# Spreading the background sums of weights differently over the slots of POOL's queue, in a fused encoder step

## The chip, the cores and the metric

One core of one Trainium2 chip runs the whole program in one launch. The metric is the device time in microseconds (us), the median of the runs shown. Engines are named as in the profile: PE (TensorE), DVE (VectorE), ACT (ScalarE), POOL (GpSimd), SP (SyncE, which here only issues DMAs).

## What is computed

One layer of a hybrid encoder for 512 prompt tokens and 32 tokens of a running stream, 544 in all, 1024 features, float32:

```python
xn = rms_norm(x, g_mix)
u, q, k, v, gates = split(xn @ w_in)               # one projection, 4096 columns
y_pool = multiscale_pool(u)                        # causal window means 2/4/8/16, minus the token
y_sb = stick_breaking(q, k, v)                     # 8 heads of 64, strictly causal
merged = sig(gate_a) * (y_pool @ w_pool_up) + sig(gate_b) * (y_sb @ w_sb_up)
x = x + merged @ w_out
x = x + square(relu(rms_norm(x, g_mlp) @ w_up)) @ w_down      # D_FF = 4096
x = x + sigmoid(rms_norm(x, g_ple) @ w_ple_gate) * (p @ w_ple_proj)
y = rms_norm(x, g_final)
```

## The kernel before, in words

Activations stay on chip, features on the partitions, 544 tokens along the free dimension. Weights come from HBM in tiles of 128 x 1024 float32 (512 KB), and each is split by ACT (the rounded part, w_hi, L845 and L853) and DVE (the rest, w_lo, L1812 and L1820), so that three PE products stand for one float32 product. SP loads the tiles (L651 up to the output projection, L680 to L690 behind it). Until the MLP there are two raw buffers, and ACT and DVE split three tiles ahead of PE.

**Stages.** Four "pairs" come first: each projects eight weight tiles (PE L1345, L1348, L1351) and runs two attention heads in between. Then come the mixer (the pooling and attention outputs projected up, the sample tokens' attention), the output projection, the MLP in four chunks, and the gated embedding.

**A head.** For head g PE makes the scores (L1381), ACT the softplus chain (L921 to L925), DVE closes it (L1898). POOL then zeroes what is not causal in four 128x128 blocks (mask_diagonals, L767, counted in spm_done). ACT and DVE split the masked matrix (L930, L1913), and PE sums it (L1394). ACT takes the exponential (L938). POOL masks it again (L767, counted in pm_done), ACT and DVE split it (L943, L1919), and PE multiplies it by v (L1420). Every engine's program is in order. In the same queues stand the weight splits and the q, k and v parts of the next pair.

**The background sums.** From the MLP on, groups of weights are multiplied in a Strassen-Winograd form: seven products stand for eight, and four of the seven left operands are sums of quarters of the weights (S1 to S4). POOL makes these sums with DMAs from HBM to HBM, in the Internal tensor sums_t: a plain copy (L782), and transfers that add to their destination (accumulate, L789). Each of the 16 groups (SUM_GROUPS: up 0, up 1, dn 0, dn 1, up 2, ..., ple 1) takes four steps (SUM_STEPS): four copies, then two additions, then one, then one, each transfer 512 KB, 128 in all. Steps are run in slots. Slot k first waits until every transfer of the slots before it has landed (sum_copies, a wait on sums_in for sums_made(k - 1)), then issues its copies and its additions. Slots 0 to 7 stand in POOL's queue right behind the second mask of heads 0 to 7. For even heads the pooling branch's window_sums (L742 to L747) stand between the two masks. Its window_mean (L757 to L760) stands behind the slot, but for head 6, where it stands ahead of the second mask. Slots 8 to 18 follow the heads; but for slot 8 they are paced by PE's progress (paces, waits on full). In the kernel before, group i begins in slot i. SP loads a sum of group i only when the slot of its last step has landed (L679).

Of the kernel before, what the change touches and what calls it, by code (L numbers as in the profile page):

```python
# [19 lines left out]
HEADS = 8  # L20
# [66 lines left out]
SUM_STEPS = ((("S1", "A21"), ("S3", "A21"), ("S2", "A11"), ("S4", "A12")), (("S1", "A22"), ("S3", "A11")),  # L87
             (("S2", "S1"),), (("S4", "S2"),))

SUM_GROUPS = tuple((what, 2 * c + e) for c in range(CHUNKS) for what in ("up", "dn") if what == "up" or c < SEVENS  # L90
                   for e in range(2)) + (("ple", 0), ("ple", 1))

SUM_PAD = 16

# [63 lines left out]
def t_dn(c, s, e):  # L158
    return T_MLP + c * T_CHUNK + 2 * T_UP + 2 * s + e


def t_down(c, q):
    return T_MLP + c * T_CHUNK + 2 * T_UP + q


def t_ple(g, s):
    return T_PLE + g * (T_UP + 1) + PLE_PLACE[g][s]


def t_group(g, s):  # L170
    return t_up(g, s) if g < UP_GROUPS else t_ple(g - UP_GROUPS, s)
# [31 lines left out]
def group_side(name):  # L203

    if name[0] == "dn":
        return ("dn", 2 * name[1] + name[3]), SIDES[name[2]]
    if name[0] in ("down", "proj", "p"):
        return None
    g, what = name
    return ("up", g) if g < UP_GROUPS else ("ple", g - UP_GROUPS), what  # L210


def stored_tile(name):

    if name[0] == "down":
        return T_MLP + 16 * name[1] + 8 + name[2]
    if name[0] == "proj":
        return T_MLP + 16 * CHUNKS + 5 * name[1] + 4
    (stage, g), what = group_side(name)
    return quarter_tile(stage, g, what)  # L220
# [77 lines left out]
def hybrid_step_kernel(nc, w_tiles, x_t, p_t, ck_t, cv, state_t, w_grp, vecs,  # L298
# [5 lines left out]
    with ctx:  # L304
# [3 lines left out]
        def sem(name):  # L308
            return ctx.enter_context(nc.semaphore(name))
# [156 lines left out]
        def raw_at(n):  # L466

            return (n + RAW_RING) % RAW_BUFS

        def raw_buf(n):  # L470
            b = raw_at(n)
            return raw[:, b, :] if b < RAW_RING else raw_more[:, b - RAW_RING, :]
# [23 lines left out]
        def tokens(i):  # L496
            return slice(i * HALF, (i + 1) * HALF)
# [24 lines left out]
        sums_in = sem("sums_in")  # L522
# [98 lines left out]

        def sum_slot(k):

            return [(i, k - i) for i in range(max(0, k - len(SUM_STEPS) + 1), min(k + 1, len(SUM_GROUPS)))]

        def sums_made(k):

            return 16 * sum(len(SUM_STEPS[step]) for j in range(k + 1) for _, step in sum_slot(j))
# [7 lines left out]
        @block.sync  # L636
        def _(sp):

            first = (("w", 0), ("x", 0), ("w", 2), ("x", 1), ("x", 2), ("x", 3), ("w", 1), ("x", 4), ("w", 3),
                     ("x", 5), ("x", 6), ("x", 7))  # L640
            for what, n in first:
                if what == "x":
                    sp.dma_start(xt[:, n, :], x_t[n, :, :]).then_inc(x_in[n], 16)
                else:
                    t, part = n // 2, slice(n % 2 * D_MODEL // 2, (n % 2 + 1) * D_MODEL // 2)
                    sp.dma_start(raw[:, t, part], w_tiles[t, :, part]).then_inc(half_in[n] if n < 3 else raw_in[1], 16)

            with sp.Fori(1, T_OUT // RAW_RING + 1) as r:
                for s in range(RAW_RING):
                    sp.wait_ge(wlo_done, r * RAW_RING + (s - RAW_RING + 1))  # L650
                    sp.dma_start(raw[:, s, :], w_tiles[r * RAW_RING + s, :, :]).then_inc(raw_in[s], 16)  # L651

            def wait_free(n):

                if n < RAW_BUFS - RAW_RING:
                    sp.wait_ge(yblo_done, 2)
                elif n < RAW_BUFS:
                    sp.wait_ge(wlo_done, T_MLP - RAW_RING + raw_at(n) + 1)
                else:
                    name = STAGED_LOADS[n - RAW_BUFS]  # L660
                    if name[0] == "dn":
                        sp.wait_ge(wlo_done, t_dn(*name[1:]) + 1)
                    elif name[0] == "down":
                        sp.wait_ge(wlo_done, t_down(name[1], name[2]) + 1)
                    elif name[0] == "p":
                        sp.wait_ge(ptlo_done, name[1] + 1)
                    elif name[0] == "proj":
                        sp.wait_ge(wlo_done, t_ple(name[1], T_UP) + 1)
                    else:
                        g, what = name  # L670
                        sp.wait_ge(wlo_done, t_group(g, SIDES.index(what)) + 1)

            def staged(n):
                name = STAGED_LOADS[n]
                wait_free(n)
                group, what = group_side(name) or (None, None)
                if what in SUMS:
                    nth = SUM_GROUPS.index(group)
                    sp.wait_ge(sums_in, sums_made(nth + len(SUM_STEPS) - 1))  # L679
                    sp.dma_start(raw_buf(n), sums_t[len(SUMS) * nth + SUMS.index(what), :, :])\  # L680
                        .then_inc(raw_in[raw_at(n)], 16)
                elif name[0] == "p":
                    sp.dma_start(raw_buf(n)[:, 0:TOK], p_t[:, name[1], :]).then_inc(raw_in[raw_at(n)], 16)
                else:
                    sp.dma_start(raw_buf(n), w_tiles[stored_tile(name), :, :]).then_inc(raw_in[raw_at(n)], 16)


            for j, t in enumerate(range(T_OUT + RAW_RING, T_MLP)):
                sp.wait_ge(wlo_done, t - RAW_RING + 1)
                sp.dma_start(raw[:, t % RAW_RING, :], w_tiles[t, :, :]).then_inc(raw_in[t % RAW_RING], 16)  # L690
                for n in range(2 * j, min(2 * j + 2, RAW_BUFS - RAW_RING)):
                    staged(n)
            for n in range(RAW_BUFS - RAW_RING, len(STAGED_LOADS)):
                staged(n)
            for nth, i in enumerate((1, 0)):

                for m in (4, 2, 0, 6) if nth else (0, 4, 2, 6):
                    if m == 0:
                        sp.wait_ge(fin_pool, 2 * nth + 2)
                    else:  # L700
                        sp.wait_ge(fin_done, len(BY_DVE) * nth + BY_DVE.index(m) + 1)
                    for two in range(2):
                        sp.dma_start(y_t[m + two, :, tokens(i)], xt[:, m + two, tokens(i)]).then_inc(out_done, 16)
            sp.wait_ge(out_done, 16 * 2 * KT)

        @block.gpsimd
        def _(pool):
# [67 lines left out]
            def sum_copies(k):  # L775

                if 0 < k:
                    pool.wait_ge(sums_in, sums_made(k - 1))
                for i, step in sum_slot(k):
                    if step == 0:  # L780
                        for what, of in SUM_STEPS[0]:
                            pool.dma_start(sum_tile(i, what), sum_tile(i, of)).then_inc(sums_in, 16)  # L782

            def sum_additions(k):

                for i, step in sum_slot(k):
                    if step:
                        for what, of in SUM_STEPS[step]:
                            pool.dma_start(sum_tile(i, what), sum_tile(i, of), accum_op=ALU.add).then_inc(sums_in, 16)  # L789
# [21 lines left out]
            paces = [(0, 0), (N_ATT, N_ATT + KT // 2), (N_OUT, N_OUT + KT // 2)]  # L811
            for c in range(CHUNKS):
                second = [NTH[("dn", c, s, 0)] for s in (0, 4)] if c < SEVENS else [NTH[("down", c, q)] for q in (0, 4)]
                paces += [(NTH[("up", 2 * c, 0)], NTH[("up", 2 * c + 1, 0)]), tuple(second)]
            for k, (copies, additions) in enumerate(paces, HEADS):
                if copies:
                    pool.wait_ge(full, copies)
                sum_copies(k)
                if copies:
                    pool.wait_ge(full, additions)  # L820
                sum_additions(k)
# [1732 lines left out]
```

## Time and profile before

| what | value |
|---|---|
| time, median of 3 runs | 772.89 us (772.16 to 772.94) |
| the profiled execution | 772.34 us, its span 770.6 us |
| granted TensorE clock, mean | 0.996 of full speed |
| PE busy | 754.8 us, 98% of the span |
| DVE, ACT, POOL busy | 556.9, 422.0, 147.2 us |
| DMA from POOL (q0) | 67.18 MB, 35.5% of 16 engines' span |
| DMA from SP (q1) | 94.16 MB, 35.6% |

The profile takes one execution. Busy PE includes matmuls that overlap in the pipeline, so its idle time is the safer reading: a few stretches at the start and the end, and hardly any between. The DMA engines' share is a mean over stretches with very different traffic.

### The profile page before, as it was taken

How to read it: one execution, taken by the hardware profiler on the slowest of the kernel's cores; microseconds unless marked ns; L12 is line 12 of the kernel's file. 1: busy time of each engine (PE TensorE's matmuls, PEld its weight loads, DVE VectorE, ACT ScalarE, POOL GpSimd, SP SyncE). 2: the span in 40 equal slices, each digit the busy share in tenths (PEclk: the TensorE clock that was granted, in tenths of full speed). 3: DMA queues.
4: the chain of work that ended last, by engine and by line, in shares of the span. 5: the costliest groups of instructions: out<-in, count | busy, mean ns of one | idle time of the engine just before them, and what ended most of it. 6: DMA issues, size and time to landing. Idle time of an engine off the chain costs nothing.

```text
span 770.6 us, 14459 instructions
## 1 busy us (share of the span) xinstructions
PE 754.8 (98%) x5902; PEld 746.2 (97%) x5902; DVE 556.9 (72%) x705; ACT 422.0 (55%) x524; POOL 147.2 (19%) x259
## 2 busy tenths in 40 slices
PE   9999999999999999999999999999999999999994
PEld 9999999999999999999999999999999999999993
DVE  6776556566567527588998669965998667677986
ACT  7545535435485442477674347634763356556575
POOL 1051342453471332021110111111101000000001
PEclk9999999999999999999999999999999999999998
DMA  7254848769779899988797989789776957342503
GB/s 242 93 181 140 233 147 224 225 193 262 218 179 265 259 242 275 292 267 262 213 299 270 236 329 251 282 232 354 207 243 201 278 185 217 105 117 66 204 1 116
DMA packets 49516, 165.78 MB, mean 215 GB/s; under 512 B 6320, under 2 KB 8368, under 8 KB 49456
## 3 DMA queue, kind: packets, MB, share of 16 engines
q1 hardware_dynamic: 28512, 94.16, 35.6%
q0 software_dynamic: 18688, 67.18, 35.5%
q10 hardware_dynamic: 2256, 3.60, 1.4%
q8 instruction: 43, 0.70, 0.4%
q14 instruction: 17, 0.14, 0.1%
HBM read 160.39 MB, written 71.63 MB: 301 GB/s over the span
## 4 chain that ended last, share of the span: by engine, by line
PE 90%; DVE 5%; ACT 3%; issue 1%; DMA 1%; SPq 0%; POOL 0%; POOLq 0%; DVEq 0%
PE psum L1646 23%; PE psum L1697 16%; PE psum L1345 14%; PE psum L1351 14%; PE psum L1348 14%; PE psum L1394 1%; PE psum L1422 1%; DMA xt<-x_t 1%; PE psum L1420 1%; PE psum L1382 1%; PE psum L1381 1%; ACT xt L1265 1%; PE psum L1401 1%; PE psum L1406 1%; ACT L879 0%
## 5 line engine op out<-in xcount | busy, mean ns | idle before, releaser
L853 ACT ACTIVATE w_hi<-raw_more 128x1024 fp32r<-128x1024 f32 x83 | 87.7, 1056 | 72.3 <-PE psum L1697 43.3
L1345 PE MATMUL psum<-a_hi,w_hi 128*128 128x272 f32 x576 | 120.6, 291 | 0.6 <-DVE w_lo L1812 0.5
L1820 DVE TENSOR_TENSOR w_lo<-raw_more,w_hi 128x1024 fp32r<-128x1024 f32 x83 | 101.1, 1222 | 26.1 <-ACT w_hi L853 25.7
L1351 PE MATMUL psum<-a_hi,w_lo 128*128 128x272 f32 x576 | 119.3, 289 | 0.0
L1348 PE MATMUL psum<-a_lo,w_hi 128*128 128x272 f32 x576 | 118.9, 288 | 0.0
L1646 PE MATMUL psum<-u_hi,w_hi 128*128 128x272 f32 x560 | 116.4, 289 | 1.0 <-ACT h_of L1097 1.0
L1646 PE MATMUL psum<-u_hi,w_lo 128*128 128x272 f32 x560 | 115.8, 289 | 0.0
L1646 PE MATMUL psum<-u_lo,w_hi 128*128 128x272 f32 x560 | 115.7, 288 | 0.0
L1345 PEld LDWEIGHTS psum<-a_hi,w_hi 128*128 128x128 f32 x576 | 90.3, 189 | 1.1 <-DVE w_lo L1812 0.7
L1348 PEld LDWEIGHTS psum<-a_lo,w_hi 128*128 128x128 f32 x576 | 90.5, 189 | 0.0
L1351 PEld LDWEIGHTS psum<-a_hi,w_lo 128*128 128x128 f32 x576 | 90.0, 189 | 0.0
L1646 PEld LDWEIGHTS psum<-u_hi,w_hi 128*128 128x128 f32 x560 | 87.9, 188 | 1.7 <-issue 1.2
L1646 PEld LDWEIGHTS psum<-u_lo,w_hi 128*128 128x128 f32 x560 | 88.3, 189 | 0.0
L1646 PEld LDWEIGHTS psum<-u_hi,w_lo 128*128 128x128 f32 x560 | 87.4, 188 | 0.0
L1812 DVE TENSOR_TENSOR w_lo<-raw,w_hi 128x1024 fp32r<-128x1024 f32 x41 | 51.2, 1250 | 43.3 <-ACT w_hi L845 43.1
L1820 DVE TENSOR_TENSOR w_lo<-raw,w_hi 128x1024 fp32r<-128x1024 f32 x44 | 53.6, 1222 | 19.2 <-ACT w_hi L853 12.3
L789 POOL DMA_DIRECT2D sums_t<-sums_t x32 | 27.5, 1013 | 207.1 <-PE psum L1646 87.9
L1348 PE MATMUL psum<-b_lo,w_hi 128*128 128x272 f32 x304 | 62.9, 288 | 0.0
L853 ACT ACTIVATE w_hi<-raw 128x1024 fp32r<-128x1024 f32 x39 | 41.2, 1056 | 36.0 <-PE psum L1697 21.6
L1345 PE MATMUL psum<-b_hi,w_hi 128*128 128x272 f32 x288 | 60.0, 290 | 0.0
L782 POOL DMA_DIRECT2D sums_t<-w_tiles x64 | 33.6, 535 | 135.5 <-DMA sums_t<-w_tiles 97.7
L1351 PE MATMUL psum<-b_hi,w_lo 128*128 128x272 f32 x288 | 59.4, 287 | 0.0
(287 smaller groups left out, 1553.0 us busy)
## 6 DMA issues: line engine op xcount, KB each, us to landing
sums_t<-w_tiles POOLq DMA_DIRECT2D x96, 512.0 KB, 8.2
raw<-w_tiles SPq DMA_DIRECT2D x63, 512.0 KB, 4.4
raw_more<-sums_t SPq DMA_DIRECT2D x42, 512.0 KB, 5.8
raw_more<-w_tiles SPq DMA_DIRECT2D x41, 512.0 KB, 4.5
sums_t<-sums_t POOLq DMA_DIRECT2D x32, 512.0 KB, 11.1
raw<-sums_t SPq DMA_DIRECT2D x22, 512.0 KB, 6.0
xt<-x_t SPq DMA_DIRECT2D x8, 272.0 KB, 5.7
y_t<-xt SPq DMA_DIRECT2D x16, 136.0 KB, 1.9
```

What stands on the lines that cost most here:

```text
L782: pool.dma_start(sum_tile(i, what), sum_tile(i, of)).then_inc(sums_in, 16)
L789: pool.dma_start(sum_tile(i, what), sum_tile(i, of), accum_op=ALU.add).then_inc(sums_in, 16)
L853: act.activation(w_hi[:, t % W_RING, :, :].rearrange("p k c -> p (k c)"), src, ACT.Copy)\
L1265: act.activation(x, x, ACT.Copy, scale=g_fin[:, m:m + 1]).then_inc(xg_last, 1)
L1345: pe.matmul(base[:, h, :], w_hi[:, s, wk, :], at(hi, k, h * HALF, (h + 1) * HALF), start=(opens and q == 0), stop=False, skip_group_check= ...
L1348: pe.matmul(base[:, h, :], w_hi[:, s, wk, :], at(lo, k, h * HALF, (h + 1) * HALF), start=False, stop=False, skip_group_check=True)
L1351: mm = pe.matmul(base[:, h, :], w_lo[:, s, wk, :], at(hi, k, h * HALF, (h + 1) * HALF), start=False, stop=(closes and q == len(ks) - 1), s ...
L1381: pe.matmul(z, b_lo[:, keys], b_hi[:, both], start=(b != 3), stop=False, skip_group_check=True)
L1646: mm = pe.matmul(out[:, two, :], w_part[:, t % W_RING, 2 * k + two, :], u_part[:, op, k, :], start=(OPENS[s] and k == 0 and w_part is w_hi ...
L1697: mm = pe.matmul(out[:, two, :], w_part[:, t % W_RING, 2 * k + two, :], h_part[:, i * HALF:(i + 1) * HALF], start=(OPENS[s] and k == 0 and ...
L1812: dve.tensor_tensor(w_lo[:, s, :, :].rearrange("p k c -> p (k c)"), raw[:, t % RAW_RING, :], w_hi[:, s, :, :].rearrange("p k c -> p (k c)" ...
L1820: dve.tensor_tensor(w_lo[:, t % W_RING, :, :].rearrange("p k c -> p (k c)"), src, w_hi[:, t % W_RING, :, :].rearrange("p k c -> p (k c)"), ...
```

## The change

A table BEGINS says in which slot each group begins, in place of its own number. Groups 0 to 8 begin in slots 0, 1, 2, 2, 3, 3, 4, 5, 5, groups 9 and 10 in slots 7 and 9, and groups 11 to 15 in their own slots 11 to 15, as before. The last step of each group stays three slots behind its first, and the waits follow the table. The 128 transfers are the same ones. Slots 0 to 18 stand where they stood, each with its wait for the slot before.

```diff
+BEGINS = (0, 1, 2, 2, 3, 3, 4, 5, 5, 7, 9, 11, 12, 13, 14, 15)
+SLOTS = BEGINS[-1] + len(SUM_STEPS)
...
         def sum_slot(k):
 
-            return [(i, k - i) for i in range(max(0, k - len(SUM_STEPS) + 1), min(k + 1, len(SUM_GROUPS)))]
+            return [(i, k - at) for i, at in enumerate(BEGINS) if 0 <= k - at < len(SUM_STEPS)]
...
                     nth = SUM_GROUPS.index(group)
-                    sp.wait_ge(sums_in, sums_made(nth + len(SUM_STEPS) - 1))
+                    sp.wait_ge(sums_in, sums_made(BEGINS[nth] + len(SUM_STEPS) - 1))
...
-            for k, (copies, additions) in enumerate(paces, HEADS):
+            for k, (copies, additions) in zip(range(HEADS, SLOTS), paces):
```

Transfers of each slot, copies + additions, counted from the code:

| slot | 0 | 1 | 2 | 3 | 4 | 5 | 6 | 7 | 8 | 9 | 10 | 11 |
|---|---|---|---|---|---|---|---|---|---|---|---|---|
| before | 4+0 | 4+2 | 4+3 | 4+4 | 4+4 | 4+4 | 4+4 | 4+4 | 4+4 | 4+4 | 4+4 | 4+4 |
| after | 4+0 | 4+2 | 8+3 | 8+6 | 4+7 | 8+6 | 0+7 | 4+3 | 0+4 | 4+1 | 0+3 | 4+1 |

## Rows read from the trace of the kernel before

**Rows 1.** The page: TensorE's busy time and share of the span.

```profile
PE 754.8 (98%) x5902; PEld 746.2 (97%) x5902; DVE 556.9 (72%) x705; ACT 422.0 (55%) x524; POOL 147.2 (19%) x259
```

**Rows 2.** PE's waits: who waited for what, us in total, times, longest.

```profile
PE psum L1345 <- issue: 1.1, 1, 1.1
PE psum L1646 <- ACT h_of L1097: 1.0, 1, 1.0
```

**Rows 3.** POOL's timeline in heads 2 to 7 (start, us, instructions; idle before).

```profile
111.51 2.07 POOL L782 DMA_DIRECT2D sums_t<-w_tiles  x4
...
140.45 2.15 POOL L782 DMA_DIRECT2D sums_t<-w_tiles  x4
...
152.17 1.95 POOL L767 TENSOR_SCALAR_AFFINE_SELECT work<-work 128x128 f32<-128x128 f32 x4 [6.14 <-DVE work L1898]
...
169.95 2.09 POOL L782 DMA_DIRECT2D sums_t<-w_tiles  x4
...
177.35 1.18 POOL L760 TENSOR_TENSOR upad<-gates,upad 128x559 f32<-128x559 f32 x1
183.69 1.03 POOL L767 TENSOR_SCALAR_AFFINE_SELECT work<-work 128x128 f32<-128x128 f32 x4 [5.16 <-DVE work L1898]
...
198.88 2.16 POOL L782 DMA_DIRECT2D sums_t<-w_tiles  x4
...
210.60 1.95 POOL L767 TENSOR_SCALAR_AFFINE_SELECT work<-work 128x128 f32<-128x128 f32 x4 [6.14 <-DVE work L1898]
...
228.33 2.16 POOL L782 DMA_DIRECT2D sums_t<-w_tiles  x4
...
244.37 1.02 POOL L767 TENSOR_SCALAR_AFFINE_SELECT work<-work 128x128 f32<-128x128 f32 x4 [10.46 <-DVE work L1898]
...
256.03 2.09 POOL L782 DMA_DIRECT2D sums_t<-w_tiles  x4
...
267.74 0.44 POOL L807 TENSOR_SCALAR_AFFINE_SELECT work<-work 32x256 f32<-32x256 f32 x1 [6.18 <-DVE work L2111]
```

**Rows 4.** Slots 0 to 3 to landing: stretch, engines' busy, PEclk, DMA share, GB/s.

```profile
52.90:62.40 9.50, 9.50 (x73) 9.23 (x71) 5.18 (x5) 4.63 (x5) 6.35 (x8) 1.00 0.85 300
...
82.00:98.70 16.70, 16.70 (x131) 16.53 (x131) 10.61 (x16) 9.06 (x10) 7.08 (x14) 1.00 0.93 262
98.70:102.00 3.30, 3.30 (x29) 3.30 (x28) 3.30 (x3) 1.20 (x2) 2.49 (x2) 1.00 0.12 37
111.50:129.60 18.10, 18.10 (x143) 17.93 (x141) 10.67 (x14) 8.65 (x8) 8.71 (x15) 1.00 0.95 258
...
140.40:163.00 22.60, 22.60 (x179) 22.43 (x178) 14.91 (x20) 10.29 (x11) 13.26 (x18) 1.00 0.95 254
```

**Rows 5.** POOL's timeline behind the heads: slots 8, 9 and 10.

```profile
280.25 2.09 POOL L782 DMA_DIRECT2D sums_t<-w_tiles  x4 [4.04 <-DMA sums_t<-w_tiles]
...
303.32 2.07 POOL L782 DMA_DIRECT2D sums_t<-w_tiles  x4 [17.57 <-DMA sums_t<-w_tiles]
...
330.50 1.57 POOL L782 DMA_DIRECT2D sums_t<-w_tiles  x3 [21.71 <-DMA sums_t<-w_tiles]
```

**Rows 6.** Behind head 5's first mask: ACT's and DVE's timelines, and PE's chain.

```profile
184.75 1.27 ACT L930 ACTIVATE b_hi<-work 128x1280 fp32r<-128x1280 f32 x1 [3.79 <-POOL work L767]
...
194.32 0.72 DVE L1857 TENSOR_TENSOR ev<-psum,rn 128x544 f32<-128x544 f32 x1 [0.20 <-PE psum L1351]
...
196.60 1.24 ACT L938 ACTIVATE work<-psum 128x1280 f32<-128x1280 f32 x1 [0.24 <-PE psum L1394]
...
200.28 1.49 DVE L1919 TENSOR_TENSOR b_lo<-work,b_hi 128x1280 fp32r<-128x1280 f32 x1
...
202.63 0.24 PE psum L1420
```

**Rows 7.** The page: POOL's DMA queue, its packets, MB, share of 16 engines.

```profile
q0 software_dynamic: 18688, 67.18, 35.5%
```

**Rows 8.** Weight loads (L651): to landing, from 129 to 140 us, then 141 to 163.

```profile
DMA to landing us min/median/max: 3.5/3.8/4.2
...
DMA to landing us min/median/max: 3.5/8.4/8.7
```

## The prediction

> **What bounds the kernel now.** I read the page first: PE is busy for 754.8 of 770.6 us [rows 1]. Then PE's own waits, where the reader should look for a DMA or a weight tile: between the first weights and the last stage PE waits 1.1 us once for its own issue and 1.0 us once for ACT [rows 2], and the list names no load and no sum. So even if the change frees all the DMA time between the heads and the MLP, at most 2.1 us can come back there, and neither wait names a DMA. The question is what it puts into the heads. POOL's timeline answers that [rows 3]: slots 3 to 7 are issued at 140.45, 169.95, 198.88, 228.33 and 256.03, some 29.2 us apart, and none has to wait for the slot before it, since their eight transfers have landed by then. In slot 3 the DMA engines are busy for 0.95 of 22.6 us [rows 4]. Some 6.5 us are left over per head.
>
> A difference of less than 0.2% (1.5 us) can't be told from no change.
>
> **What a slot costs.** The stretches to landing are 9.5, 16.7, 18.1 and 22.6 us for 4+0, 4+2, 4+3 and 4+4 transfers (copies + additions), weight loads between them included [rows 4]; behind slot 1 the share falls to 0.12, so the stretch ends where I put it. Four additions take 22.6 - 9.5 = 13.1 us, 3.3 us each. A copy takes at most 9.5 / 4 = 2.4; I leave 1.1 us for the start of a slot and take 2.1. Check: 4+2 gives 1.1 + 8.4 + 6.6 = 16.1 (16.7 in the row), 4+3 gives 19.4 (18.1). Then:
> - slot 2, 8+3: 1.1 + 16.8 + 9.9 = 27.8 us
> - slots 3 and 5, 8+6: 1.1 + 16.8 + 19.8 = 37.7 us
> - slot 4, 4+7: 1.1 + 8.4 + 23.1 = 32.6 us
> - slot 6, 0+7: 1.1 + 23.1 = 24.2 us
>
> **When the slots start.** Slot 2 starts at 111.5 and has landed at 139.3, 1.1 us before slot 3: no wait. Slot 3 starts at 140.45 and lands at 178.2, but slot 4 is due at 169.95, so POOL waits 8.2 us. Slot 4 lands at 178.2 + 32.6 = 210.8 (slot 5 was due at 198.9), slot 5 at 210.8 + 37.7 = 248.5 (slot 6 at 228.3), slot 6 at 248.5 + 24.2 = 272.7 (slot 7 at 256.0).
>
> **What stands behind the waiting POOL.** Its issues take 2.15 us for four [rows 3], 0.54 each; the additions I price the same. In the same rows:
> - Slot 3 issues 14 in 7.6 us, until 148.0; head 4's first mask is at 152.17. Nothing is late.
> - Slot 4: 178.2, 11 issues (5.9), and window_mean. The latter ended at 177.35 + 1.18 = 178.5, which is 8.6 us behind 169.95 with eight issues (4.3) in between, so it takes 4.3 itself. Head 5's first mask comes at 188.4, not 183.7: 4.7 late.
> - Slot 5: 210.8 + 14 x 0.54 = 218.4, for head 6's first mask at 210.6: 7.8 late in all, 3.1 more than before it.
> - Slot 6: 248.5 + 3.8 = 252.3, for head 7's at 244.4: 7.9.
> - Slot 7: 272.7 + 7 x 0.54 = 276.5, for the sample tokens' mask (L807) at 267.7: 8.8.
> These are not added up: each is measured against the unshifted time, so the largest is the total.
>
> **Does a late mask reach PE?** The chain behind head 5 [rows 6]: ACT takes the masked matrix at 184.75, when POOL releases it. Behind it in DVE's queue is the next pair's k (L1857), for which DVE sat idle for just 0.20 us; ACT's exponential (L938) had sat idle for 0.24. DVE's split ends at 200.28 + 1.49 = 201.77, and PE uses it at 202.63: 0.86 us. So the chain has some 0.9 us to give, perhaps 0.3 less at the sample tokens' mask. I take 8.8 - 1.0 = 7.8 us on PE. Each late mask also holds up the weight splits behind it in ACT's and DVE's queues; they are part of the same chain, and I add nothing.
>
> **The rest.** Weight loads: with the queue empty they land in 3.8 us, beside the sums in 8.4 (medians) [rows 8]. In the new kernel the queue is hardly empty from 111 to 290 us, so about one load of four takes 4.6 us more. Two raw buffers are loaded ahead, and while POOL is late ACT's use of them is too, so I take nothing, and 2 us at the worst. The loads behind the heads meet fewer sums (4+1 in slot 9 where 4+4 stood); since PE waited for none of them, that gives nothing. SP's waits for finished sums (L679) come true in the same slots as before or in earlier ones (group 4 in slot 6, before in slot 7; groups 11 to 15 unchanged), and the first sums, of slots 3 and 4, land at 178 and 211 us, long before the MLP.
>
> **Sum.** 772.34 (the profiled execution, 0.55 us below the median) + 7.8 = 780.1; against the median 780.7. I give 780.5.
>
> **Bounds of the one unshown price**, a slot of 11 or 14 transfers. From below: the queue's 128 transfers take 35.5% of 770.6 = 273.6 us of the engines, 2.14 each [rows 7]. Slot 3 would take 22.6 + 6 x 2.14 = 35.4, slot 4 29.0, slot 5 35.4, slot 6 20.5: then slot 4 starts at 175.9 (mask 2.4 late), slot 5 at 204.9 (1.9 late), slot 7 at 260.8 (nothing late). That is 2.4 us late, and 1.4 past the slack: 774.3. From above: slots 8 and 9 of eight transfers took 303.32 - 280.25 = 23.1 and 330.50 - 303.32 = 27.2 us, and slot 7 took 24.2 [rows 3, 5]. By 24.2 / 22.6 = 1.07 slots 3 to 6 take 141.5 instead of 132.2: 9.3 us more, 789.8. By 27.2 / 22.6 = 1.2 it would be 27 us more, 807. The slots to price run in the heads, where slot 3 stands, so I keep to its 22.6. A gain is excluded by nothing but rows 2: 2.1 us.
>
> **The rivals.**
> - **More in flight hides the waits, no change.** The rows have the engines 0.95 busy with eight transfers [rows 4], which speaks against it. It would hold if that share is mostly waiting for receipts that overlap with more transfers: 14 would then have to land in under 29.5 us, 2.1 us each, against 2.8 in slot 3. 772.9. The Trainium skill says so in "DMA: Bandwidth & Descriptors", in the anatomy of a DMA from GpSimd: a fixed 2.0 us, mostly the write's receipt, plus bytes over 436 GB/s. By that page, as an estimate, 14 transfers behind one another with one receipt take 2 + 14 x 1.2 = 18.8 us, and no slot would be late. Slot 3's eight took 22.6 us, where the page's estimate is 11.6, so the trace doesn't agree.
> - **The slack is larger than it looks.** PE's sums (L1394) of head 5 began some 5 us later than the mask allowed. If the queues' reordering gives that slack to the rest, only lateness over 6 us counts: 8.8 - 6 = 2.8, and the time 775.7; by the lower price 774.3.
> - **The queue chokes.** With 14 outstanding, POOL's issue may itself block, or the transfers slow as in slot 9 [rows 5]; POOL is then late by 18 us or more, as in the 1.07 case, and the time 790 to 807.
> - **Faster: the relief counts.** If the two PE waits [rows 2] are held by DMA traffic (the 1.1 us of issue stands at the end of the pairs) and the slots land within 29 us (2.1 us each, as above), the time is 770.8 to 771.5. It decides only if no slot is late.
>
> **How the numbers follow.** The chain of late masks 0.66; the larger slack or the lower price 0.12; the choked queue 0.12; no change 0.07; faster 0.03. Slower has 0.66 + 0.12 + 0.12 = 0.90. The range goes from 774.5 (about the lower price) to 789.0 (just under the 1.07 case); outside it lie the same, the faster, and the worst of the choke, about 0.18.
>
> **What would show it.** In the profile after: POOL's L782 (and L789 in slot 6, which has no copies) waiting for DMA sums_t in heads 4 to 7, by 8, 5 to 8, 12 and 9 us; L767 idle no longer before heads 5 and 6; ACT's L930 waiting for L767 longer, PE with new waits on DVE's b_lo (L1913, L1919) or w_lo, some 8 us in all, between 188 and 280 us; DMA share about 1.0 from 112 to 290 us and lower from 290 to 360; the MLP's stretches as long as before. It is wrong if slot 3 lands before 170 us, if L767 is late and PE doesn't wait, or if PE's new waits lie behind the heads.

## The result and the profile after

The changed kernel takes 798.26 us (median of 6 runs, 797.25 to 799.65), the kernel before 773.88 in the same comparison. The ratio is 1.0313, with a 95% interval of 1.0288 to 1.0338: slower by 3.1%. I had forecast slower, but 780.5 us, and the time lies outside my range. The profiled execution takes 798.11 us, its span 796.4, 25.8 more than before. Line numbers from here on are those of the changed kernel, 4 higher than before: the slots' copies are L786, their additions L793, the masks L771, window_mean ends in L764. In the runs further down an edit can shift them by a few lines more.

First POOL's timeline of the changed kernel, in heads 4 to 7; it answers to [rows 3].

```profile
178.61 2.09 POOL L786 DMA_DIRECT2D sums_t<-w_tiles  x4 [8.56 <-DMA sums_t<-w_tiles]
...
188.56 1.18 POOL L764 TENSOR_TENSOR upad<-gates,upad 128x559 f32<-128x559 f32 x1
189.69 1.02 POOL L771 TENSOR_SCALAR_AFFINE_SELECT work<-work 128x128 f32<-128x128 f32 x4
...
213.60 4.18 POOL L786 DMA_DIRECT2D sums_t<-w_tiles  x8 [9.16 <-DMA sums_t<-w_tiles]
...
220.96 2.92 POOL L771 TENSOR_SCALAR_AFFINE_SELECT work<-work 128x128 f32<-128x128 f32 x4
225.68 0.64 POOL L746 DMA_DIRECT2D pool_t<-upad  x1 [1.80 <-DVE upad L1977]
...
249.59 1.18 POOL L764 TENSOR_TENSOR upad<-gates,upad 128x559 f32<-128x559 f32 x1 [14.62 <-DMA pool_t<-upad]
250.72 1.03 POOL L771 TENSOR_SCALAR_AFFINE_SELECT work<-work 128x128 f32<-128x128 f32 x4
251.69 2.60 POOL L793 DMA_DIRECT2D sums_t<-sums_t  x3
...
268.49 1.03 POOL L771 TENSOR_SCALAR_AFFINE_SELECT work<-work 128x128 f32<-128x128 f32 x4 [10.87 <-DVE work L1902]
...
280.13 2.09 POOL L786 DMA_DIRECT2D sums_t<-w_tiles  x4
...
291.83 0.45 POOL L811 TENSOR_SCALAR_AFFINE_SELECT work<-work 32x256 f32<-32x256 f32 x1 [7.06 <-DVE work L2115]
```

Slots 4 and 5 wait for the transfers of the slot before, 8.6 and 9.2 us, as expected. Slots 6 and 7, for which I had expected 12 and 9 us, don't wait (251.69 and 280.13): when POOL comes to them, the transfers have landed. The row to look at is 249.59: window_mean of head 6 waits 14.6 us for "pool_t<-upad". This is the small store of the pooling state (L746, L747), two DMAs of 7.5 KB. window_mean overwrites the rows that they read, so its last step waits for them, and the second mask of head 6 stands behind it. Set against [rows 3], the lateness grows in steps: head 5's first mask 189.69 for 183.69, 6.0 us; head 6's first mask starts at 220.96 and ends at 223.88, where before it ended at 210.60 + 1.95 = 212.55, 11.3; head 7's first mask 268.49 for 244.37, 24.1; the sample tokens' mask 291.83 for 267.74, 24.1.

PE's waits of the changed kernel, which answer to [rows 2]:

```profile
PE psum L1330 <- DVE mean_lo L1984: 13.5, 1, 13.5
PE psum L1424 <- DVE b_lo L1923: 4.9, 2, 4.6
```

And the chain that ended last, at the MLP's first product by w_down, before (L1697) and after (L1701):

```profile
399.83 1.25 PE psum L1697 x10
```

```profile
423.94 1.12 PE psum L1701 x9
```

That is 24.1 us again. So all of the loss arises before 270 us, and nothing of it comes back behind the heads, though the DMA engines have less to do there: from 340 to 360 us their share is 0.47, where it was 0.89 before in the same stretch. PE had waited for none of that traffic.

PE's two gaps and a short third one make 4.6 + 13.5 + 0.3 = 18.4 us of the 24.1. The rest shows in stretches of 2 us around the gaps, with the columns of [rows 4]; (x8) behind PE's busy time counts its matmuls, and the last three columns are the granted clock, the DMA share and GB/s:

```profile
206.00:208.00 2.00, 0.68 (x2) 0.58 (x3) 1.97 (x3) 0.00 (x0) 0.00 (x0) 0.68 1.02 289
208.00:210.00 2.00, 2.00 (x9) 1.90 (x8) 0.15 (x2) 0.00 (x0) 0.00 (x0) 0.50 1.08 283
210.00:212.00 2.00, 2.00 (x8) 1.81 (x8) 1.35 (x2) 0.00 (x0) 0.00 (x0) 0.50 0.40 137
212.00:214.00 2.00, 2.00 (x12) 2.00 (x12) 0.00 (x0) 1.65 (x2) 0.40 (x1) 0.61 0.05 14
...
256.00:258.00 2.00, 2.00 (x8) 1.81 (x8) 0.96 (x2) 0.12 (x1) 1.62 (x2) 0.52 1.03 287
258.00:260.00 2.00, 2.00 (x16) 1.91 (x16) 1.62 (x3) 0.71 (x1) 0.00 (x0) 1.00 1.07 254
```

Behind the first gap the granted clock is at its lower level (1.2 GHz), and 8 or 9 matmuls are done in 2 us where 16 are at 2.4 GHz. What this costs is read from the start of the same four matmuls before and after. Before:

```profile
202.47 0.40 PE L1420 MATMUL psum<-b_hi 128*128 128x512 f32 x1
...
205.76 0.42 PE L1345 MATMUL psum<-a_hi,w_hi 128*128 128x272 f32 x2
...
231.90 0.29 PE L1326 MATMUL psum<-mean_hi,b_hi 128*128 128x272 f32 x1
...
233.88 0.34 PE L1326 MATMUL psum<-b_lo,b_hi 128*128 128x272 f32 x1
```

After:

```profile
207.32 0.80 PE L1424 MATMUL psum<-b_hi 128*128 128x512 f32 x1 [4.55 <-DVE b_lo L1923]
...
213.54 0.43 PE L1349 MATMUL psum<-a_hi,w_hi 128*128 128x272 f32 x2
...
253.67 0.56 PE L1330 MATMUL psum<-mean_hi,b_hi 128*128 128x272 f32 x1 [13.48 <-DVE mean_lo L1984]
...
258.01 0.34 PE L1330 MATMUL psum<-b_lo,b_hi 128*128 128x272 f32 x1
```

The first pair is 4.9 us apart, behind the first gap. The second, where the clock is back, is 7.8 apart: 2.9 lost at the lower clock. The third is 21.8 apart, behind the second gap, and the fourth 24.1: 2.4 more, of which 0.3 is the third gap and 2.0 the clock. So the clock costs some 5.0 us. The gaps and the clock are 23.4 of the 24.1 us; of the rest, 0.3 us is a pause near 225 us and 0.2 stood ahead of the first gap.

### The profile page after: what moved, and what is told of

Same layout as the page of the kernel before. It is cut to its first block, busy times and chain, and to the rows that moved or that the text cites. A ratio compares the mean times of both kernels' runs of the same rounds, so it can differ in the third digit from the quotient of the medians.

```text
span 796.4 us, 14459 instructions
## 1 busy us (share of the span) xinstructions
PE 759.9 (95%) x5902; PEld 749.8 (94%) x5902; DVE 556.8 (70%) x705; ACT 422.2 (53%) x524; POOL 145.9 (18%) x259
## 4 chain that ended last, share of the span: by engine, by line
PE 75%; DMA 11%; DVE 5%; POOL 3%; ACT 3%; issue 1%; SPq 0%; POOLq 0%; DVEq 0%
PE psum L1650 22%; PE psum L1701 16%; PE psum L1349 11%; PE psum L1355 10%; PE psum L1352 10%; DMA sums_t<-w_tiles 8%; DMA pool_t<-upad 3%; POOL sums_t L793 1%; POOL sums_t L786 1%; PE psum L1398 1%; DMA xt<-x_t 1%; ACT xt L1269 1%; PE psum L1424 0%; ACT L883 0%; PE psum L1426 0%
## 5 line engine op out<-in xcount | busy, mean ns | idle before, releaser
L793 POOL DMA_DIRECT2D sums_t<-sums_t x32 | 27.2, 1062 | 258.4 <-PE psum L1650 90.9
L857 ACT ACTIVATE w_hi<-raw 128x1024 fp32r<-128x1024 f32 x39 | 41.2, 1056 | 36.0 <-PE psum L1701 21.7
L849 ACT ACTIVATE w_hi<-raw 128x1024 fp32r<-128x1024 f32 x46 | 48.1, 1051 | 18.4 <-DMA raw<-w_tiles 9.4
## 6 DMA issues: line engine op xcount, KB each, us to landing
sums_t<-sums_t POOLq DMA_DIRECT2D x32, 512.0 KB, 11.3
```

What stands on the lines that cost most here:

```text
L849: act.activation(w_hi[:, s, :, :].rearrange("p k c -> p (k c)"), raw[:, t % RAW_RING, :], ACT.Copy).then_inc(whi_done, 1)
L857: act.activation(w_hi[:, t % W_RING, :, :].rearrange("p k c -> p (k c)"), src, ACT.Copy)\
```

## The experiments

Ratios are to the kernel before in the same comparison. Theory A: the wait for the state's store is the larger part of the loss. Theory B: the waits between slots are all of it. Theory C, later: part of it is TensorE's clock behind a gap.

**The stores from ACT's queue.** The changed kernel, with

```diff
-                pool.dma_start(pool_t[0, :, g, :], ...).then_inc(pool_out, 16)
-                pool.dma_start(pool_t[1, :, g, :], ...).then_inc(pool_out, 16)
...
                 act.activation(v_parts[:, :, V_HI, :], o_heads, ACT.Copy).then_inc(vhi_done, 1)
+                act.wait_ge(taken, 4 + i * S1_PER)
...
+                act.dma_start(pool_t[0, :, i, :], ...).then_inc(pool_out, 16)
+                act.dma_start(pool_t[1, :, i, :], ...).then_inc(pool_out, 16)
```

> The changed kernel, with the eight small stores of the pooling state (pool_t, 7.5 KB each) issued by ACT right behind its copy of the v parts, not by POOL. Theory A (the stores stand in POOL's DMA queue behind the 14 transfers of slot 5, so window_mean of head 6, which waits for them, is held until slot 5 has landed): the wait of 14.6 us on pool_t and PE's wait of 13.5 us go. What is left is the shift that was there before it, 11.1 us at head 6's exponential: about 785 us. Theory B (only the waits between slots matter, and the mean would be late for another reason): 798 us, as in the changed kernel.

Measured: 789.61 us (788.04 to 790.92), ratio 1.0189 (1.0164 to 1.0215). PE's wait of 13.5 us is down to 4.6, where theory A had it at zero and the time at 785 us. The first fence is that kernel's POOL timeline, the second its answer on the tile pool_t, the third that of the changed kernel.

```profile
239.83 1.18 POOL L762 TENSOR_TENSOR upad<-gates,upad 128x559 f32<-128x559 f32 x1 [6.12 <-DMA pool_t<-upad]
250.69 2.60 POOL L791 DMA_DIRECT2D sums_t<-sums_t  x3 [7.65 <-DMA sums_t<-w_tiles]
```

```profile
DMA to landing us min/median/max: 1.6/7.1/14.9
```

```profile
DMA to landing us min/median/max: 2.2/12.4/23.1
```

From POOL's queue the stores landed in 23.1 us, at the end of slot 5's transfers (DMA share 0.85 from 246 to 248 us, 0.06 in the next 2 us). From ACT's they took 14.9 us and landed some 11 us before slot 5 had (250.69). So a queue of its own helps here, as theory A has it, but 7.5 KB still take 15 us when the sums fill the DMA engines. The Trainium skill ("DMA: Bandwidth & Descriptors", "Queues, rings and completion order") says that each DMA engine takes turns between the queues it has work for, a packet at a time; a store in another queue landing ahead of the transfers agrees with that. It gives no time for a turn, and no run here shows one.

**One group early.** Only BEGINS is different:

```diff
-BEGINS = (0, 1, 2, 2, 3, 3, 4, 5, 5, 7, 9, 11, 12, 13, 14, 15)
+BEGINS = (0, 1, 2, 3, 4, 5, 5, 7, 8, 9, 10, 11, 12, 13, 14, 15)
```

> Only group 6 begins early: BEGINS = (0, 1, 2, 3, 4, 5, 5, 7, 8, ..., 15), so that slot 5 has 8 copies and 4 additions, slot 6 none and 6. Slot 5 is priced 1.1 + 16.8 + 13.2 = 31.1 us, from 198.9 to 230.0, while slot 6 is due at 228.3 and the next mask at 244: no mask behind a slot is late. Theory B (only waits between slots): 773.9, no change. Theory A (the stores behind slot 5's transfers): window_mean, ready at 223.7, ends at about 231.2 and head 6's second mask comes 4 to 5 us late; PE stands still for about 4 us: 777 to 778, and up to 3 us more if PE's clock falls behind that gap, as it did in the changed kernel: 781 at the most.

Measured: 779.57 us (778.54 to 780.10), ratio 1.0057 (1.0038 to 1.0075); 5 us lost, where theory B had none. Its POOL timeline:

```profile
223.84 0.22 POOL L762 TENSOR_TENSOR gates<-gates,invc 128x16 f32<-128x16 f32 x1
230.81 1.18 POOL L764 TENSOR_TENSOR upad<-gates,upad 128x559 f32<-128x559 f32 x1 [6.75 <-DMA pool_t<-upad]
231.94 1.03 POOL L771 TENSOR_SCALAR_AFFINE_SELECT work<-work 128x128 f32<-128x128 f32 x4
```

No slot in the heads waits; the store alone makes the mask 4.6 us late (227.35 before). PE stands still for 2.4 us, and the clock falls behind that.

**One group early, the stores from ACT.** Both edits together.

> The same table as in the run with one group early, and the stores of the pooling state issued by ACT. Theory A: no late mask and no store behind the sums, so the time of before, 773 to 775. Theory B: the same as the run with one group early, whatever that is. If the twelve transfers themselves disturb the heads (weight loads, say), it stays above 776.

Measured: 778.22 us (774.78 to 780.06), ratio 1.0043 (1.0025 to 1.0062). A miss for theory A as I had put it (773 to 775): the store takes 15.4 us from ACT's queue, where it took 15.3 from POOL's, and window_mean waits 6.6 us for it. With twelve transfers in slot 5 the queue makes no difference, with fourteen it made 8 us. This run fits theory B as well; the next one tells them apart.

**One group early, the state copied first.** Here window_mean doesn't wait for the store. POOL still waits for older stores before it overwrites the copy, and for all of them at the end, but the trace shows no idle time for either:

```diff
...
+                link(pool.tensor_copy(state_out[:, g % 2, 0, :], u[:, U_STATE - STATE:U_STATE]))
+                link(pool.tensor_copy(state_out[:, g % 2, 1, :], u[:, PADW - STATE:PADW]))
-                pool.dma_start(pool_t[0, :, g, :], u[:, U_STATE - STATE:U_STATE]).then_inc(pool_out, 16)
...
+                pool.dma_start(pool_t[0, :, g, :], state_out[:, g % 2, 0, :]).then_inc(pool_out, 16)
...
-                pool.wait_ge(pool_out, 32 * (g + 1))
...
```

> The table with one group early (slot 5 with 8 copies and 4 additions), and the state stored from a copy, with no wait in window_mean. No slot is late enough for a mask, and no store is waited for. Theory A: the time of before, 773 to 775.5, and no gap of PE near 233 us. If the twelve transfers disturb the heads in another way (weight loads), it stays at 777 or more.

Measured: 773.36 us (772.71 to 774.27), ratio 1.0003 (0.9992 to 1.0013). The same twelve transfers, the same slots, and no loss. The stores still took up to 13.8 us here; nothing stood behind them. POOL's timeline:

```profile
224.78 1.18 POOL L768 TENSOR_TENSOR upad<-gates,upad 128x559 f32<-128x559 f32 x1
227.55 1.03 POOL L775 TENSOR_SCALAR_AFFINE_SELECT work<-work 128x128 f32<-128x128 f32 x4 [1.59 <-ACT work L947]
```

The mask is back at 227.55, waiting for ACT. This shows the wait on the store to be the cause of the 5 us.

**Two groups early, the state copied first.** BEGINS = (0, 1, 2, 2, 4, 5, 5, 7, 8, ..., 15).

> BEGINS = (0, 1, 2, 2, 4, 5, 5, 7, 8, ..., 15), the state stored from a copy with no wait in window_mean. Slot 2 has 8+3 transfers (27.8 us by my prices), slot 3 0+6 (20.9), slot 4 4+3, slot 5 8+4 (31.1), slot 6 0+5. No slot ends more than 2 us behind the next one's due time, and no store is waited for. Theory A: 773 to 775, as before. If crowding alone disturbs the heads: 777 or more.

Measured: 773.90 us (772.58 to 774.90), ratio 0.9985 (0.9966 to 1.0003): no difference that can be told. Slots with eight copies fit as long as nothing on PE's path waits for a slot or a store, and they bring nothing. (Slot 6 waited 2.2 us for slot 5 here, and 2.3 us in the run before; neither cost anything.)

**The changed kernel, the state copied first.**

> The changed kernel, but POOL first copies the 15 + 15 columns of the pooling state to a small buffer of their own and stores them from there, so that window_mean needs no wait for the stores. Theory A (the wait for the stores is the larger part of the loss, whichever queue they go through): PE's wait before L1330 (13.5 us) goes to zero, and what is left is the lateness that stands behind the waits between slots 3 to 5, 11.1 us at head 6's exponential: 784 to 787. Theory B (the waits between slots are all): 798.

Measured: 795.60 us (794.85 to 795.92), ratio 1.0288 (1.0270 to 1.0306). This is the surprise: PE's wait of 13.5 us is gone, and only 3 us came back. PE's waits:

```profile
PE psum L1429 <- DVE b_lo L1928: 6.1, 3, 4.6
PE psum L1545 <- DMA cvn<-cv: 4.6, 1, 4.6
...
PE psum L1335 <- DVE mean_lo L1989: 1.2, 1, 1.2
```

Now PE waits for the cached keys and values (ckt, cvn, 512 KB each). ACT issues them at 266.2 and 266.8, 12 us earlier than in the changed kernel (277.9 and 278.5), into the middle of slot 6. The values land in 11.6 us, in place of 5.3. The clock falls again behind that gap, here for longer: this fence has stretches of 2 us of that kernel.

```profile
278.00:280.00 2.00, 1.55 (x7) 1.55 (x8) 0.00 (x0) 0.00 (x0) 2.00 (x4) 0.50 0.76 260
282.00:284.00 2.00, 2.00 (x13) 1.77 (x13) 0.00 (x0) 0.84 (x2) 0.59 (x1) 0.50 0.91 305
286.00:288.00 2.00, 2.00 (x11) 2.00 (x11) 0.99 (x2) 1.75 (x1) 0.44 (x1) 0.55 1.08 272
288.00:290.00 2.00, 2.00 (x18) 1.97 (x16) 1.45 (x2) 0.00 (x0) 0.00 (x0) 1.00 1.05 188
```

Where the time went is read from PE's matmuls again. The first row is of the kernel before, the others are of this run:

```profile
259.98 0.47 PE L1420 MATMUL psum<-b_hi 128*128 128x512 f32 x1
```

```profile
272.40 0.48 PE L1429 MATMUL psum<-b_hi 128*128 128x512 f32 x1
...
278.45 3.68 PE L1545 MATMUL psum<-qbd,ckt 128*128 128x64 f32 x16 [4.58 <-DMA cvn<-cv]
```

In head 7 this kernel is 12.4 us behind, where the changed kernel is 24.1 behind (284.08): 11.7 us came back there, and 773.5 + 12.4 = 786 is what theory A had forecast. Then 9.0 us were lost again, 4.7 in the gap and 4.3 behind it at the lower clock; at the MLP it is 21.4 behind (421.28 for 399.83). Slots 6 and 7 now wait 11.5 and 9.4 us, close to the 12 and 9 of my forecast.

Both theories fall here in their plain form. The store's wait is a real loss, and so are the slots' waits. But with the store's wait gone, the same saturated DMA engines hold up the next transfer that someone waits for.

**Slot 3 alone.** BEGINS = (0, 1, 2, 2, 3, 3, 6, 7, 8, ..., 15).

> BEGINS = (0, 1, 2, 2, 3, 3, 6, 7, 8, ..., 15): slots 2 and 3 as in the changed kernel (8+3 and 8+6), then slot 4 with 0+7 and slot 5 with 0+4. Only slot 4 has to wait (until 178.6), its 7 issues take 3.8 us and window_mean 4.3, so head 5's first mask starts at about 187, 3 us late; slack 0.9. Slack as I priced it: PE stands still for about 2 us, 776, or 779 if the clock falls behind it. The larger slack (6 us before PE's sums): 774.

Measured: 779.46 us (778.22 to 780.06), ratio 1.0076 (1.0056 to 1.0096). POOL's timeline, and PE's waits:

```profile
179.64 2.57 POOL L793 DMA_DIRECT2D sums_t<-sums_t  x3 [9.72 <-DMA sums_t<-w_tiles]
...
183.41 3.80 POOL L761 TENSOR_SCALAR gates<-gates 128x551 f32<-128x551 f32 x1
...
187.46 1.18 POOL L764 TENSOR_TENSOR upad<-gates,upad 128x559 f32<-128x559 f32 x1
188.59 1.03 POOL L771 TENSOR_SCALAR_AFFINE_SELECT work<-work 128x128 f32<-128x128 f32 x4
```

```profile
PE psum L1424 <- DVE b_lo L1923: 3.7, 1, 3.7
```

This is the wait between slots by itself. The mask is 188.59 - 183.69 = 4.9 us late, and PE stands still for 3.7: the chain has 1.2 us to give, not the 6 of my rival. The clock falls behind that gap too (0.50 from 206 to 212 us), which brings the loss to 6 us.

**Half of each addition.** The changed kernel, but each addition moves 64 of the 128 partitions, so half of every sum is left out:

```diff
-                            pool.dma_start(sum_tile(i, what), sum_tile(i, of), accum_op=ALU.add)...
+                            pool.dma_start(sum_tile(i, what)[0:P // 2], sum_tile(i, of)[0:P // 2], accum_op=ALU.add)...
```

> The changed kernel with its table, its waits and its 128 transfers, but each addition moves 64 partitions of 128 (256 KB); half of each sum is left out. Both theories: the slots' transfer time is the cause, not the number of issues on POOL: slots 3 and 5 take 1.1 + 16.8 + 9.9 = 27.8 us, slot 4 21.1, all under the 29 us between slots; the store of head 6 lands at 227, some 3 us behind the time it was needed: 773 to 777. A theory by which 14 issues, or 14 transfers in the queue, hold up POOL by themselves: over 785.

Measured: 776.37 us (775.70 to 778.45), ratio 1.0022 (1.0008 to 1.0036). The 14 issues on POOL are all there, and no slot waits any more. So the time that the transfers take is the cause, and not their number. The store is still waited for, 5.8 us, and PE's gaps are 1.4 and 1.1 us. Behind these two the clock stays at 1.00.

**The clock: matmuls that nobody reads in the gap.** The kernel with one group early, with 11 of them on PE ahead of the wait:

```diff
+                    pe.wait_ge(vlo_done, PAIRS)
+                    for _ in range(11):
+                        pe.matmul(psum[:, 7, 0:P], negone[:, :].bitcast(F32), negone[:, :].bitcast(F32), ...)
                     group(0)
```

> The kernel with one group early, and 11 matmuls of 128x128 float32 by negone that nobody reads, in PE's queue ahead of the first pooling group of the last pair, where PE stood still for 2.4 us; they take about 0.22 us each, 2.4 us in all. Theory C (part of the loss is the clock of TensorE, granted at half behind such a gap for some 6 us): the clock stays at 1.00, and the time falls by about 3 us, to 776.5, though work is added. Rival: the gap alone is the loss, and the fall of the clock has another cause: 779.6 or a little more.

Measured: 777.49 us (776.86 to 782.03), ratio 1.0067 (1.0039 to 1.0096). Its partner had been timed beside other runs of the kernel before, so both were timed once more, side by side.

> The kernel with one group early once more, beside its own copy with the filler, since the two ran in different comparisons (779.57 over 774.52, and 777.49 over 773.5) and their ratios to before, 1.0057 and 1.0067, don't tell them apart. Expected as before: 5 us over before.

> One group early with the 11 unread matmuls in the gap, again. Theory C (the clock behind a gap is part of the loss): the clock keeps 1.00 and the time is 1.5 to 3 us below its partner in this comparison. Rival (the gap is all): no difference, or slower by up to 1 us.

Measured: 778.82 us (778.42 to 781.26) without, 780.19 us (776.86 to 781.83) with the matmuls; ratios 1.0065 (1.0041 to 1.0089) and 1.0075 (1.0048 to 1.0102). The times don't show theory C. In the profiled executions the clock does keep 1.00 with them, in both runs, and the MLP's first L1701 or L1705 product starts 2.1 us earlier:

```profile
406.66 42.34 PE psum L1701 x336
```

```profile
404.58 42.34 PE psum L1705 x336
```

But that execution took 776.86 us, the fastest of its six, and four of the others took 779.55 or more. The last attempt put 58 such matmuls into the long gap of the changed kernel.

> The changed kernel with 58 unread matmuls (0.22 us each, 12.8 us) in PE's queue ahead of the first pooling group of the last pair, where PE stood still for 13.5 us. The wait on the stores stays. Theory C: PE keeps its clock there and does the 3.6 us behind the gap at 2.4 GHz, not at 1.2: 1.8 us less, 796.4. Rival: 798 or more.

Measured: 798.77 us (796.84 to 801.30), ratio 1.0314 (1.0278 to 1.0349): no gain. PE still had gaps of 1.9 and 1.0 us behind the added work, and the clock fell there as before. What the lower clock costs is read from the traces (5.0 us in the changed kernel); that it could be avoided is not shown.

## Why the prediction was wrong

**Right.** The relief behind the heads is worth nothing: 24.1 us of shift at the sample tokens' mask, 24.1 at the MLP. The slots' prices nearly hold: slot 3 was priced 37.7 us and took 178.61 - 140.51 = 38.1, slot 4 32.6 and took 35.0, slot 5 37.7 and took some 36 (to the end of the store's wait). Slots 4 and 5 waited 8.6 and 9.2 us; I had said 8 and 5 to 8. (The slots before are 28.9 us apart in the mean, and not 29.2.) The waits of 12 and 9 us for slots 6 and 7 didn't come in the changed kernel, but did where the store's wait was gone. The rival with more transfers in flight and no loss is out: slot 3's 14 transfers took 38.1 us. The estimate of 18.8 us by the Trainium skill ("DMA: Bandwidth & Descriptors", "Anatomy of one DMA") is about half of that. The rival with 6 us of slack is out by the run with slot 3 alone. (PE's sums of head 5 began not 5 but 6.5 us later than the mask allowed, at 194.05 for 187.55, and it gave nothing.)

**The step that failed** is the list of what stands behind the waiting POOL. For slot 5 I wrote "210.8 + 14 x 0.54 = 218.4, for head 6's first mask at 210.6: 7.8 late in all", and took that mask as the end of the matter. A few instructions further on in the same queue, window_mean waits for its own two small stores, and these share the DMA engines with slot 5's transfers. In the kernel before they never showed as a wait, but only just: head 6's stores landed within 8.0 us, and window_mean came to its last step 8.8 us after the second was issued (214.97 and 223.72). So I priced no DMA but the sums and the weight loads. That wait is 14.6 us on POOL, and PE stands still for 13.5 us at mean_lo, a wait that my list of signs didn't name. By an estimate some 2 of the 13.5 us are the late mask's and not the store's, since PE still has gaps of 1.2 and 1.0 us there with the state copied first. The runs with one group early show it alone: 5 us lost with the wait, none without.

**A term that was left out** is TensorE's clock. I took PE's lateness as the loss; the trace has 5.0 us more, from working at 1.2 GHz behind the two gaps. The slack that I took off (1.0 us) was about right (1.2).

**Sizes that were off.** Head 5's mask was 6.0 us late, not 4.7: window_mean runs beside the DMA issues, and its L761 takes 3.9 us behind seven additions where it took 2.9 behind four. Head 6's first mask ended 11.3 us late, not 7.8: the 35.0 us of slot 4, and four blocks that took 2.9 us beside the issues, where they had taken 1.95. By these alone (11.3 in place of 7.8) the forecast would have been 3.5 us higher, 784, still inside my range.

**The rival that came nearest** is the choked queue, with 790 to 807 us at 0.12: POOL late by 18 us or more. Its time was right by luck, its mechanism wasn't. Slots 3 to 5 took no more than 1.07 of their price, and POOL's issue was never blocked. The transfers that came late were the small ones, and with the state copied first the cached values.

**Left open.** How the time of a small store comes about under this load (15 us from ACT's queue, 23 from POOL's). Also the 1.7 us by which the spans differ beyond the 24.1: they lie behind POOL's last product, which still starts 24.1 us later (789.00 for 764.90). A version that beats the kernel before wasn't found, and the traces offer none in this part: PE waits for no sum and for no weight between the heads and the MLP.

## What to carry to other kernels

Before work is moved into a stage, list every wait on a DMA in that stage, the smallest too, and price each as if the DMA engines were full. A store of 7.5 KB took 23 us here, and the engine that waited for it stood in the main chain. A wait that is never seen in a profile is only a wait whose transfer is early; when one is removed, ask which DMA is waited for next. And an engine that has no gaps has nothing to gain from relief elsewhere.

## What was not expected of the hardware

- A store of 7.5 KB to HBM landed in 1.6 us at the best. When POOL's transfers filled the DMA engines (share 1.0) it took 14.9 to 15.4 us from ACT's queue, and 15.3 and 23.1 us from POOL's, behind 12 and 14 transfers; weight loads of 512 KB land in 8.4 us beside them [rows 8].
- The granted clock fell to its lower level in or behind each PE gap of 2.4, 3.7, 4.6 and 13.5 us, for some 3 to 14 us. Of short gaps in succession the runs give no rule: around 1.4 and 1.1 us it stayed at 1.00 (half of each addition), behind 1.2 and 1.0 us, at the same place in PE's program, it fell (the changed kernel with the state copied).
- POOL's vector work slows beside its own DMA issues: the same TENSOR_SCALAR took 2.6 us right behind three additions, 2.9 behind four and 3.8 to 3.9 behind seven, with four copies ahead of them or with none.
